# State update ahead of the gated convolution, sums over four units, `qkd` turned a strip later, decay rows a head ahead, high parts of the weights first

## The reference

```python
N_META, N_HEADS, DK, DV = 16, 8, 128, 256          # D_MODEL 2048, SEQ 256, DEC_BATCH 8, D_FF 5632

def mlstm_chunk(state, inp):
    c_prev, n_prev, m_prev = state
    ...
    w_ts = jnp.exp(dmat - m_t[..., None])
    s = jnp.einsum('bhtd,bhsd->bhts', q, k) * w_ts
    decay = jnp.exp(b + m_prev[..., None] - m_t)
    num = decay[..., None] * jnp.einsum('bhtd,bhdv->bhtv', q, c_prev) + jnp.einsum('bhts,bhsv->bhtv', s, v)
    den = decay * jnp.einsum('bhtd,bhd->bht', q, n_prev) + jnp.sum(s, axis=-1)
    h = num / jnp.maximum(jnp.abs(den), jnp.exp(-m_t))[..., None]
    ...
    c_new = carry[..., None, None] * c_prev + jnp.einsum('bhs,bhsd,bhsv->bhdv', g, k, v)
    n_new = carry[..., None] * n_prev + jnp.einsum('bhs,bhsd->bhd', g, k)
    return (c_new, n_new, m_last), h

def block(x, ...):
    h = rmsnorm(x, norm1_g)
    z = h @ w_in
    ...
    conv_out, sc = causal_dwconv(cg * u, sc0, w_shortconv)
    a_out = bg * conv_out
    ...
    b_out = jax.nn.sigmoid(o) * hb
    mix = jax.nn.sigmoid(g_a) * a_out + jax.nn.sigmoid(g_b) * b_out
    x = x + mix @ w_out
    h2 = rmsnorm(x, norm2_g)
    up, fc = causal_dwconv(h2 @ w_up, fc0, w_ffconv)
    return x + (jax.nn.silu(up[..., D_FF:]) * up[..., :D_FF]) @ w_down, c, n, m, sc, fc
```

## Time and profile before

| | us |
|---|---|
| median of 3 runs | 1788.23 |
| lowest, highest | 1785.95, 1793.69 |
| the profiled execution | 1791.13 |
| its span, first to last instruction | 1789.4 |
| PE busy | 1737.3 |
| DVE, ACT, POOL busy | 1142.8, 746.0, 429.4 |

### The profile page before, as it was taken

The page is one execution under the profiler, slowest core; times in us unless marked ns, Lnnn a source line. Parts: engine busy times, 40 slices in busy tenths (PEclk is TensorE's granted clock), DMA queues, the critical chain, the costliest instruction groups (busy, mean ns, idle before and its releaser), DMA issues.

```text
span 1789.4 us, 37065 instructions
## 1 busy us (share of the span) xinstructions
PE 1737.3 (97%) x13817; PEld 1723.2 (96%) x13817; DVE 1142.8 (64%) x1825; ACT 746.0 (42%) x872; POOL 429.4 (24%) x378
## 2 busy tenths in 40 slices
PE   6799999999999999999999999999999999999997
PEld 5699999999999999999999999999999999999997
DVE  3575655756565575656677777777555777777553
ACT  6433443343333333334344554454333333334443
POOL 3251422315142141414211222222000222222000
PEclk9899999999999999999999999999999999999999
DMA  7767677675777767677766566666666565666653
GB/s 182 148 160 200 166 209 193 187 193 152 200 178 200 195 175 184 167 200 174 206 176 175 168 177 175 176 176 174 182 179 187 171 178 173 177 175 179 177 170 109
DMA packets 590568, 318.77 MB, mean 178 GB/s; under 512 B 16737, under 2 KB 585569, under 8 KB 588409
## 3 DMA queue, kind: packets, MB, share of 16 engines
q1 hardware_dynamic: 575504, 292.85, 60.4%
q10 hardware_dynamic: 14609, 23.30, 4.8%
q0 software_dynamic: 368, 1.31, 0.2%
HBM read 305.07 MB, written 12.78 MB: 178 GB/s over the span
## 4 chain that ended last, share of the span: by engine, by line
PE 89%; DVE 4%; issue 3%; DMA 2%; ACT 1%; ACTq 0%; POOL 0%; DVEq 0%; POOLq 0%
PE strip L1189 85%; PE aux L1274 1%; ACT w_hi L544 1%; PE aux L1143 1%; DVE rden L951 1%; DVE w_lo L788 1%; DMA gw<-in_w_in 1%; DVE sacc L964 1%; PE aux L1278 1%; DVE sacc L968 1%; DMA rb<-scratch_rows 1%; DMA out<-m_samp 0%; PE aux L1160 0%; PE aux L1253 0%; PE strip L1143 0%
## 5 line engine op out<-in xcount | busy, mean ns | idle before, releaser
L1189 PE MATMUL strip<-xh,w_hi 128*128 128x266 f32 (+2 forms) x3456 | 998.6, 289 | 1.0 <-DVE w_lo L788 1.0
L1189 PE MATMUL strip<-xh,w_lo 128*128 128x266 f32 (+2 forms) x3456 | 997.5, 289 | 0.0
L1189 PE MATMUL strip<-xl,w_hi 128*128 128x266 f32 (+2 forms) x3456 | 996.4, 288 | 0.0
L788 DVE TENSOR_TENSOR w_lo<-w_raw,w_hi 128x1024 fp32r<-128x1024 f32 x560 | 707.8, 1265 | 431.1 <-ACT w_hi L544 429.6
L544 ACT ACTIVATE w_hi<-w_raw 128x1024 fp32r<-128x1024 f32 x560 | 592.2, 1060 | 874.8 <-PE strip L1189 869.1
L1189 PEld LDWEIGHTS strip<-xh,w_hi 128*128 128x128 f32 x3456 | 658.1, 190 | 1.8 <-DVE w_lo L788 1.3
L1189 PEld LDWEIGHTS strip<-xl,w_hi 128*128 128x128 f32 x3456 | 656.9, 190 | 0.3
L1189 PEld LDWEIGHTS strip<-xh,w_lo 128*128 128x128 f32 x3456 | 656.7, 190 | 0.0
L1189 PE MATMUL strip<-hh,w_hi 128*128 128x264 f32 x704 | 201.5, 286 | 0.0
L1189 PE MATMUL strip<-hh,w_lo 128*128 128x264 f32 x704 | 200.5, 285 | 0.0
L1189 PE MATMUL strip<-hl,w_hi 128*128 128x264 f32 x704 | 200.3, 285 | 0.0
(11 more groups left out here) (256 smaller groups left out, 1186.3 us busy)
## 6 DMA issues: line engine op xcount, KB each, us to landing
w_raw<-in_w_in SPq DMA_DIRECT2D x256, 512.0 KB, 4.2
w_raw<-in_w_up SPq DMA_DIRECT2D x176, 512.0 KB, 4.0
w_raw<-in_w_down SPq DMA_DIRECT2D x64, 512.0 KB, 4.1
w_raw<-in_w_out SPq DMA_DIRECT2D x32, 512.0 KB, 4.3
w_raw<-in_w_down SPq DMA_DIRECT2D x32, 384.0 KB, 3.4
c_st<-in_state_mlstm_C ACTq DMA_DIRECT2D x8, 1024.0 KB, 9.7
out<-c_st ACTq DMA_DIRECT2D x8, 1024.0 KB, 6.9
rb<-scratch_rows ACTq DMA_DIRECT2D x8, 270.0 KB, 5.5
```

Source lines behind the costliest of these rows:

```text
L788: v.tensor_tensor(w_lo[:, slot, :], w_raw[:, slot, :], w_hi[:, slot, :].bitcast(f32), ALU.subtract).then_inc(lo_done, 1)
L1189: mm = pe.matmul(bank[b][:, 0:c1 - c0], wt[:, slot, w], xt[:, k0 + k, c0:c1], start=(first and k == 0 and t == 0), stop=(last and k == kk ...
```

## The change

- **POOL**: in tile 0 the state update comes ahead of `a_gated = bs * cv`.
- **DVE**: the eight sums go in pairs behind steps 16 to 19; the `n` sums (`sn`, `qp`, `n_new`) from unit 8 to 13; the samples' end from 20 to 22; the split of the mix from 22 to 24.
- **PE**: `qkd` is turned behind strip 5 instead of 4, into other columns of `aux[3]`, with a wait for `kv_done`; behind strip 6 it waits for `vs_done` instead; the samples' numerator comes behind strip 10 instead of 9. In each unit the 16 matmuls on `w_hi` come first and wait for `hi_done`, then the 8 on `w_lo`, which wait for `lo_done`. Waits for tiles stand only in the first loop.
- **ACT**: exp and copies are one block at unit 9; `qkd24` is copied at unit 11, the read back at unit 12. `rb` of head n + 1 is fetched at unit 28 of head n, `c_st` at unit 2 of the next `front`; `c_st` is stored at unit 22 instead of 24. In head 0 `rb` waits for the store of the rows alone; `m_row` and `m_samp` count on `m_stored`, for which ACT waits behind step 8, ahead of the load of `c_st`. Head 0's `back` and head 1's `front` stand ahead of the loop.

```diff
-                    g.wait_ge(evacuated, out_of(s + 2))
-                    g.wait_ge(conv_step, j * 5 + 5)
-                    g.tensor_tensor(a_gated[:, :], bs[:, :], cv[:, :], ALU.mult).then_inc(a_done, 1)
...
+                    g.wait_ge(evacuated, out_of(s + 2))
+                    g.wait_ge(conv_step, j * 5 + 5)
+                    g.tensor_tensor(a_gated[:, :], bs[:, :], cv[:, :], ALU.mult).then_inc(a_done, 1)
...
-                         .then_inc(rows_stored, 16)
+                         .then_inc(m_stored, 16)
                         with nc.allow_non_contiguous_dma(reason="64 stabilisers"):
-                            act.dma_start(s_m[0].rearrange("b h -> h b"), m_samp[:, :]).then_inc(rows_stored, 16)
-                    if i == 7:
-
-                        if not first:
-                            act.wait_ge(h_step, n * HST)
-                            act.wait_ge(hs_step, n * HSS)
-                            act.wait_ge(n_step, n * 2)
-                            act.wait_ge(c_updated, n * (JG // 2))
-                            act.wait_ge(c_stored, n * 16)
-                            act.wait_ge(pc_stored, n * 16)
-                        else:
-                            act.wait_ge(pre_step, 6)
-                            act.wait_ge(rows_stored, 48)
+                            act.dma_start(s_m[0].rearrange("b h -> h b"), m_samp[:, :]).then_inc(m_stored, 16)
+                    if not first and i == 2:
+                        act.wait_ge(c_updated, n * (JG // 2))
+                        act.wait_ge(c_stored, n * 16)
+                        act.dma_start(c_st[:, :, :].rearrange("p j v -> p (j v)"), state_C_v[n]).then_inc(c_in, 16)
+                    if first and i == 7:
+                        act.wait_ge(rows_stored, 16)
                         act.dma_start(rb[:, :], scratch_rows[bass.ds(n, 1), :].broadcast_to([P, RW]))\
                          .then_inc(rb_in, 16)
-                        act.dma_start(c_st[:, :, :].rearrange("p j v -> p (j v)"), state_C_v[n]).then_inc(c_in, 16)
...
-                    if i == 8:
+                    if first and i == 8:
+                        act.wait_ge(pre_step, 6)
+                        act.wait_ge(m_stored, 32)
+                        act.dma_start(c_st[:, :, :].rearrange("p j v -> p (j v)"), state_C_v[n]).then_inc(c_in, 16)
+                    if i == 9:
                         act.wait_ge(arg_done, n + 1)
                         act.activation(wx[:, :], arg[:, :], ACT.Exp).then_inc(exp_done, 1)
-                    if i == 10:
                         act.wait_ge(kv_turned, n + 1)
-                        act.wait_ge(g3_done, n + 1)
-                        act.activation(qkd24[:, :], aux[3][0:3 * NS, P:2 * P], ACT.Copy).then_inc(vs_done, 1)
                         act.activation(v24[:, :], aux[2][0:T2 + NS, 2 * P:2 * P + DV], ACT.Copy).then_inc(vs_done, 1)
                         act.activation(v_tok[:, 0:2, 0:DV], aux[1][:, :].rearrange("p (j v) -> p j v", j=2), ACT.Copy)
+                        act.wait_ge(g3_done, n + 1)
                         for t in range(2):
                             act.activation(kg[:, t, :], aux[2][:, t * P:(t + 1) * P], ACT.Copy, scale=g3[:, t:t + 1])
                         act.activation(v_tok[0:T2, 2, 0:DV], aux[2][0:T2, 2 * P:2 * P + DV], ACT.Copy)
                         act.activation(kg[0:T2, 2, :], aux[3][0:T2, 0:P], ACT.Copy, scale=g3[0:T2, 2:3])\
                          .then_inc(kv_done, 1)
+                        act.wait_ge(vs_done, n * 2 + 1)
+                        act.dma_start(scratch_v[bass.ds(n, 1), :].rearrange("a (b v) -> (a b) v", b=NS), v24[T2:T2 + NS, :])\
+                           .then_inc(vs_stored, 16)
+                    if i == 11:
+                        act.wait_ge(qkd_turned, n + 1)
+                        act.activation(qkd24[:, :], aux[3][0:3 * NS, QC:QC + P], ACT.Copy).then_inc(vs_done, 1)
                         act.wait_ge(vs_done, n * 2 + 2)
                         act.dma_start(scratch_q_w[n], qkd24[:, :].rearrange("r (g j) -> r g j", j=JG))\
                            .then_inc(vs_stored, 16)
-                        act.dma_start(scratch_v[bass.ds(n, 1), :].rearrange("a (b v) -> (a b) v", b=NS), v24[T2:T2 + NS, :])\
-                           .then_inc(vs_stored, 16)
-                    if i == 11:
+                    if i == 12:
                         act.wait_ge(vs_stored, n * 32 + 32)
                         act.dma_start(qkd_g[:, :], scratch_q_r[n]).then_inc(vb_in, 16)
                         act.dma_start(vg[:, :], scratch_v_r[n]).then_inc(vb_in, 16)
...
-                    if i == 24:
+                    if i == 22:
                         act.wait_ge(c_updated, n * (JG // 2) + JG // 2)
                         act.dma_start(s_C_v[n], c_st[:, :, :].rearrange("p j v -> p (j v)")).then_inc(c_stored, 16)
+                    if i == 28 and not last:
+                        act.wait_ge(h_step, n * HST + HST)
+                        act.wait_ge(hs_step, n * HSS + HSS)
+                        act.wait_ge(n_step, n * 2 + 2)
+                        act.dma_start(rb[:, :], scratch_rows[bass.ds(n + 1, 1), :].broadcast_to([P, RW]))\
+                         .then_inc(rb_in, 16)
 
             front(0, first=True)
-            with act.Fori(0, H - 1) as n:
+            back(0, first=True)
+            front(1)
+            with act.Fori(1, H - 1) as n:
                 back(n)
                 front(n + 1)
-            back(H - 1)
+            back(H - 1, last=True)
...
-                        v.tensor_tensor(sn[:, :], scn[:, 2 * P:].rearrange("p (b h) -> p b h", b=NS)[:, :, bass.ds(n, 1)]
-                                        .rearrange("p b a -> p (b a)"), dec, ALU.mult).then_inc(sn_done, 1)
-                        v.wait_ge(qkd_done, n * 3 + 3)
-                        v.wait_ge(sn_done, n * 2 + 1)
-                        v.tensor_tensor(sn[:, :], sn[:, :], qkd[:, :, 1], ALU.add).then_inc(sn_done, 1)
-                        v.wait_ge(sn_done, n * 2 + 2)
-                        v.tensor_tensor(qp[:, :], q_t[:, PM:NM], sn[:, :], ALU.mult).then_inc(qn_done, 1)
...
+                    if 16 <= i < 20:
+
+                        jp = i - 16
                         sa0 = n * (JG + 1)
-                        for jg in range(JG):
-                            v.wait_ge(c_updated, n * (JG // 2) + (jg // 2 + 1))
-                            if jg < 2:
-                                v.tensor_scalar(sacc[:, jg, :], c_st[:, jg, :], qkd_g[:, jg:jg + 1], None, ALU.mult)\
+                        v.wait_ge(c_updated, n * (JG // 2) + (jp + 1))
+                        for a in range(2):
...
                             else:
                                 v.wait_ge(sacc_step, sa0 + (jg - 1))
-                                v.scalar_tensor_tensor(out=sacc[:, jg % 2, :], in0=c_st[:, jg, :],
-                                                       scalar=qkd_g[:, jg:jg + 1], in1=sacc[:, jg % 2, :],
+                                v.scalar_tensor_tensor(out=sacc[:, a, :], in0=c_st[:, jg, :],
+                                                       scalar=qkd_g[:, jg:jg + 1], in1=sacc[:, a, :],
                                                        op0=ALU.mult, op1=ALU.add).then_inc(sacc_step, 1)
-                        v.wait_ge(sacc_step, sa0 + JG)
-                        v.tensor_tensor(sacc[:, 0, :], sacc[:, 0, :], sacc[:, 1, :], ALU.add).then_inc(sacc_step, 1)
+                        if i == 19:
+                            v.wait_ge(sacc_step, sa0 + JG)
+                            v.tensor_tensor(sacc[:, 0, :], sacc[:, 0, :], sacc[:, 1, :], ALU.add).then_inc(sacc_step, 1)
...
-                    if i == 20:
+                    if i == 22:
...
-                        if (k == 22 and jj == 0) or (k == 19 and jj == 1):
+                        if (k == 24 and jj == 0) or (k == 19 and jj == 1):
...
-                pe.wait_ge(lo_done, u + 1 + RING)
+                pe.wait_ge(hi_done, u + 1)
                 for k in range(kk):
                     for at_k, sm, value in waits:
                         if at_k == k:
                             pe.wait_ge(sm, value)
                     w = slice(k * P, (k + 1) * P)
-                    for t, (wt, xt) in enumerate(((w_hi, rh), (w_hi, rl), (w_lo, rh))):
-                        mm = pe.matmul(bank[b][:, 0:c1 - c0], wt[:, slot, w], xt[:, k0 + k, c0:c1],
-                                       start=(first and k == 0 and t == 0), stop=(last and k == kk - 1 and t == 2))
+                    for t, xt in enumerate((rh, rl)):
+                        pe.matmul(bank[b][:, 0:c1 - c0], w_hi[:, slot, w], xt[:, k0 + k, c0:c1],
+                                  start=(first and k == 0 and t == 0), stop=False)
+                pe.wait_ge(lo_done, u + 1 + RING)
+                for k in range(kk):
+                    w = slice(k * P, (k + 1) * P)
```

(15 more changed lines are left out.)

28 lines of the change are left out of this document (21 added, 7 removed).

## The result

The changed kernel takes **1767.92 us** (median of 4 runs, 1766.65 to 1769.93) against 1789.24 (4 runs beside them, 1785.95 to 1793.69): ratio 0.9881, 95% interval 0.9864 to 0.9898. That is 21.3 us less, 1.2%. The forecast of 1763.4 was 4.5 us low, the time lies inside its range (1757 to 1773). The profiled execution took 1768.86, its span is 1767.1.

The account below looks back on a forecast made before the run. PE, busy 97% of the span, was taken as the bound, so only its waits and clock count. Terms 9.2 + 11.7 + 7.7 - 0.9 = 27.7 us off the profiled 1791.1 gave 1763.4, range 1757 to 1773.

Parts of the forecast that it names:

- Part 1, the sums: All heads: asking a strip later removes PE's waits for `sacc`, -11.7 us, and the slow-clock dips behind them, -7.7 us.
- the slack on DVE: Head 6: the last sums end at about 751.5 and PE asks at 753.3, so 2 us to spare.
- Part 2, head 0: Head 0: `rb` waits only for its own store, PE's 12.5 us wait becomes 4.5, strip 6 ends 9.2 us earlier.
- even at 9.2 us lands at 73.7: Head 0: `rb`, issued at about 64.5, lands by 73.7 and is no longer the last to come.
- The term of the weights: Head 0: weights issued at 63.0 take 12.5 us, unit 9's `w_hi` starts at 75.0, `kv_done` comes at 78.5.
- The clock term: Head 0, strip 6 behind PE's wait: the slow clock costs the same 1.4 us as before.
- Part 3, high parts first: All 560 units: PE begins 1.1 us earlier, nothing gained in steady state, a new 0.9 us wait for `ml`.
- Rival E: Order inside a unit slows the matmul rate; slower than before from 2.1 ns each, 1816 us at 4 ns; chance 0.04.
- B: Head 0: the rows' store counts as landed only after the small ones, gain 4.0 instead of 9.2, 1768.6 us; chance 0.15.
- A: The forecast itself: all terms as stated, rows' store counted early, 1763.4 us, own range 1758 to 1769; chance 0.67.
- C: Clock dips come of themselves, not from the waits: 7.7 us stays, 1771.1 us; chance 0.09.
- D: Sums still come after PE asks at strip 10: 11.7 and 7.7 us stay, 1782.8 us; chance 0.05.

Follow-up runs that it names:

- sums_at_once: The changed kernel with VectorE's eight sums in one go at unit 16 instead of pairs at units 16 to 19: 1766.59 us in one run.
- before_s10: The kernel before with only the later question (sums asked behind strip 10, samples' end at unit 22, mix split at 24): 1773.51 us, ratio 0.9906.
- no_small: The changed kernel without the stores of `m_row` and `m_samp` and the waits for their count (two outputs not written): 1763.14 us in one run.
- sums9: The changed kernel with PE asking for the samples' sums behind strip 9 again instead of strip 10: 1830.7 us, ratio 1.0223.

## Why the forecast held, and where it did not, by its own steps

- **Part 1, the sums**: -11.7 of wait and -7.7 of dips were forecast. Between the scores of head 1 and 7, 16.8 us went where 17.0 were to go. Right in cause, and in size with a little luck: with no wait left these six heads take 614.2 us (sums_at_once), 17.8 less than before, and head 3 took 1.0 back. That it comes from the later question alone is right too (before_s10: 16.8 us by itself). Wrong was the slack on DVE, 2 us: it is 0.3, and 2.4 us of wait came back.
- **Part 2, head 0**: the failing step is "even at 9.2 us lands at 73.7". The 9.2 of the earlier trace rows was a transfer issued after the small stores had landed; beside them it takes 14.5. I had the sign in hand, with weights at 12.5 and 19.1 us in the same stretch, used it for the weights, and gave `rb` its undisturbed time. The term of the weights was short as well. `kv_done` came at 82.6 instead of 78.5, and the timeline of ACT splits these 4.1 us: `w_hi` began at 77.5 instead of 75.0, since the weights went out 0.7 us later than before and took 13.7 us instead of 12.5, and the earlier start by part 3 did not come; exp then stood another 1.4 us for `rb`. So with `rb` at 73.7 PE would still have been late by most of it; what no_small shows is that the small stores were behind both landings. The clock term was short too: strip 6 took 8.1 us from 83.06 to 91.17, at full rate 5.9, so 2.2 instead of 1.4. And the small wait for the sums, 1.5 us, brought a dip of its own of about 1.5 us (0.25 of 3.5 and 0.17 of 4.0). From the period of head 0: 5.1 less wait at strip 5, 0.8 more of slow clock, 0.4 more wait and 1.5 more dip at the sums, -2.4 in all, where 9.3 were forecast.
- **The start**: 1.0 us of `w_lo` is gone from the list, but in this execution the scores of head 0 begin at 67.28 against 67.17, as the first `w_hi` began 1.1 us later (32.2 against 31.1). The stretch before it moves by as much from run to run (65.3 to 68.6 in the kernels here), so the profile can't show the gain.
- **Part 3, high parts first**: "nothing is gained in steady state" is wrong by 3.1 us. Over all 13,248 matmuls that is 0.23 ns each, inside the 0.3 ns of the range, but no stage has that mean: 0.9 ns less in the up stages, 0.7 more in the down stages, nothing in the heads. The 123.5 ns that I took for every matmul was itself a mean of 123.7 and 121.3. The new wait for `ml` is right, 0.8 us against 0.9, without a dip. Rival E comes true in small, in the down stages alone (1.0 us); as a slower kernel it is out.
- **The sum**: 27.7 forecast, 22.3 in the profiled executions. Head 0 lacks 6.9 us and the start 1.1, the feed-forward gave 3.1: part of the hit is that two errors of opposite sign met.
- **Rivals**: B's time, 1768.6, is what was measured, but by another mechanism: the store was counted early, as A said, and the transfer of `rb` took longer. C is out (before_s10, sums9). D is out in size: the sums did come after PE asked in two heads, but by 2.4 us in all instead of 11.7. The spread of the runs before (1786 to 1794) was laid to dips, and the changed kernel, with few of them, spreads over 3.3 us; before_s10 over 0.6.
- **The signs**: four of those that I had named failed, though the time lay in the range. The wait for `kg` is 7.4 us (named: 3 to 6), those for `sacc` 2.4 (under 1), the spacing over 1000 to 1640 us is 122.8 ns (123.5 +- 0.3), and the periods of heads 0 and 3 are above 103 us.

## What to carry to other kernels

A transfer's duration in a trace holds for what ran beside it: when an edit moves an issue, ask what is on the DMA engines at the new time, and look for stores of single numbers first, since they may be stored at the end of the kernel. When one wait in a chain goes, compute the next meeting of the same engines with every instruction in its queue counted, for a slack of a microsecond or two vanishes in a pair of operations queued ahead. A wait of PE can cost more than its length: here each of 1.4 us and more had a slow clock behind it, some 1.5 us more. Moving the question needed one strip of distance and no new work, and by itself brought 16.8 us (before_s10). And read a rate stage by stage: a mean over several stages hid that the new order gains in one and loses in another.
